# A two-layer hybrid decoder step: prompt attention and 12 of the prompt's first-MLP panels moved ahead of and between the samples' cache work

## The chip, the cores and the metric

One core of a Trainium2 chip runs one launch of the program. The time is device time in microseconds (us). Before the change it is the median of three runs: 1191.11 us, from 1184.08 to 1191.2. Everything is fp32.

## The reference

The step computes two decoder layers for one prompt of 256 tokens and for 8 samples with one new token each (1024 tokens of past in paged caches). Both groups use the same weights, but have their own conditioning vector. D is 1024, the MLP width 4096. Cut to what matters:

```python
for layer in range(2):
    for x, c in ((xp, c_prompt), (xs, c_sample)):
        shift, scale, gate = adaln(c, ada_w, ada_b)      # silu(c) @ w + b, three parts of 1024
        h = rms_norm(x, g) * (1 + scale) + shift
        if layer == 0:
            mq, mk, mv, nq, kc, vc, ks, vs, kw, vw, gt = attn_project(h, w_in, qk_g)   # 2840 columns
            # samples: keys and values are the cache pages and the new token
            o_moba = top 3 of the blocks of 256 keys by mean key, and the own block; 8 heads
            o_cmp, o_sel = compressed blocks of 32 (small MLP), and selected blocks of 64; 8 heads
            o_win = window of 512
            o = concat(o_moba, g0 * o_cmp + g1 * o_sel + g2 * o_win)
            x = x + gate * (o @ w_out)
        else:
            x = x + gate * s5_mixer(h)                   # diagonal complex state space, GLU
    for x, c in both:
        shift, scale, gate = adaln(c, mlp_ada_w, mlp_ada_b)
        h = rms_norm(x, g) * (1 + scale) + shift
        x = x + gate * (square(relu(h @ w1)) @ w2)       # 1024 -> 4096 -> 1024
```

It returns x of both groups, the new cache entries, the window state and the S5 states.

## The kernel before, in words

The program is written by hand as five instruction streams: PE (matrix products), DVE and ACT (vector and activation work), POOL (issues the weight loads), and SP (issues the cache loads). Each stream stands in the order in which it runs, and semaphores tie them. No scheduler moves anything.

Weights come through a ring of four slots of 2 MB (`ring`, `SLOTS` = 4). From the first MLP on each slot's place is cut into panels of 1 MB (`panels`). Cache pages come through 8 buffers of 256 KB (`kv`, semaphores `kv_full` and `kv_free`). Activations are kept transposed: `xT` and `hT` hold 8 blocks of 128 features by 264 columns, 256 of the prompt and 8 of the samples. In most products the weights are stationary (128x128) and the 264 columns are moved past them, so prompt and samples share one pass over the weights.

The stages, with their us in the profiled execution:

- 0 to 129: modulation of layer 0 (`ada0`) and the samples' compressed keys and values (L791).
- 129 to 266: input projection in 6 panels, samples' rows (L821) and the prompt's two halves (L827). The samples' queries are spread over partitions (L805). On DVE the loop at L1995 scores the cached MoBA keys: for each pair of pages two products of 128x512 (L2000) and a sum (L2004), 32 times. PE does the modulation of the first MLP (`ada1`, L702) beside it.
- 266 to 281: gate sums (L854), choice of blocks, softmax of the samples' MoBA branch.
- 281 to 367: `moba_pv` rounds 0 to 7 (L924), each over 8 value pages; from round 3 on POOL issues the odd pages (L548) and SP the even ones (L413). DVE does the query and key norms of the prompt (L1938 to L1956). Modulation of the S5 layer (`ada2`) runs between rounds 0 to 2; prompt attention for MoBA head pairs 0 to 3 between the later ones: `pair_scores` (L967, L968), `pair_log` (DVE L2090 to L2094), the exponential (ACT L1622), `pair_scale` (DVE L2099 to L2105), `pair_rest` on PE (turns L643, values L1006 and L1007).
- 367 to 440: 24 units of selected and window keys: four transposes (`turn_keys`, L643), then 16 small products (`score_keys`, L1061).
- 440 to 490: prompt pairs 4 to 11 (one NSA head each), with two units of selected values (`selected_pv`, L1156) in each, then window values.
- 492 to 532: output projection over all 264 columns (L1203), 8 chunks; sums of squares (L715); norm.
- 532 to 656: first MLP matrix w1 (L1219), 16 panels of 2 chunks, 8 matmuls a chunk. DVE squares the result (`squares`, L2247) and computes the S5 tables in the holes (L2262 to L2386): the angles, after ACT's sine the discretised coefficients, the masked B blocks (`times` L2299, `masked` L2309), the C table and its three lags (L2377 to L2382). `rows_turn`, `c_turn` and `b_turn(0..2)` on PE stand behind w1 panels (`mlp_first`, L1232).
- 656 to 780: second matrix w2 (L1228), 16 panels, with `b_turn(3)` and `k_turn` (L1314) behind its first groups.
- 780 to 936: S5 and GLU (L1444). 936 to 1171: MLP of layer 1, the same two loops. End at 1178.2.

## Time and profile before

| | us |
|---|---|
| median of 3 runs | 1191.11 |
| lowest, highest | 1184.08, 1191.2 |
| span of the profiled execution | 1178.2 |
| PE busy in it | 1019.0 (86%) |
| DVE busy | 423.6 (36%) |
| ACT busy | 248.7 (21%) |
| POOL busy | 137.7 (12%) |
| moved from and to HBM | 210.63 MB read, 7.48 MB written |

The span is from the first to the last instruction that the profiler recorded. The profiled execution's own time as the runs are timed isn't given apart; the median lies 12.9 us above the span. Busy times of PE are those of matmuls; weight loads (PEld) overlap them. The clock of PE is given as granted share, 1.00 or 0.50 in short stretches.

### The profile page before, as it was taken

What the parts mean: (1) busy time and instruction counts of PE and PEld (TensorE: products, weight loads), DVE (VectorE), ACT (ScalarE), POOL (GpSimd) and SP (SyncE); (2) the same over time, 40 slices, a digit from 0 to 9 for tenths busy, and PEclk for the clock granted to TensorE, in tenths of its full rate; (3) what the DMA queues carried; (4) which work ended last, traced back from release to release, by engine and by line L of the source; (5) the groups of instructions that cost most, each with busy time, mean ns of one, the idle gap of its engine ahead of it and who ended that gap; (6) DMA issues with size and microseconds to landing.
All of it is one profiled execution on the core that took longest, in us unless ns stands there. A gap on an engine that the chain in (4) does not pass through costs nothing.

```text
span 1178.2 us, 21097 instructions
## 1 busy us (share of the span) xinstructions
PE 1019.0 (86%) x8404; PEld 751.0 (64%) x8404; DVE 423.6 (36%) x901; ACT 248.7 (21%) x538; POOL 137.7 (12%) x180
## 2 busy tenths in 40 slices
PE   4867999945886869989999999974789799999998
PEld 2646533432234655667888888854668588878886
DVE  0434039887132635424993200048711300000000
ACT  3344121112033424312133320040110211100001
POOL 2000000101023210000111111111121011111110
PEclk9779989986896758998999999987799899999999
DMA  9984449999884492308544443354264344443440
GB/s 322 347 284 118 180 153 319 361 330 356 343 283 136 139 352 71 88 15 234 173 143 144 143 143 120 131 179 146 79 196 133 108 136 149 143 142 131 155 142 37
DMA packets 105580, 215.12 MB, mean 183 GB/s; under 512 B 20560, under 2 KB 53136, under 8 KB 105401
## 3 DMA queue, kind: packets, MB, share of 16 engines
q0 software_dynamic: 40160, 153.20, 38.4%
q1 hardware_dynamic: 63434, 57.81, 15.5%
q10 hardware_dynamic: 1904, 2.94, 0.7%
q8 instruction: 61, 1.00, 0.4%
q14 instruction: 21, 0.17, 0.0%
HBM read 210.63 MB, written 7.48 MB: 185 GB/s over the span
## 4 chain that ended last, share of the span: by engine, by line
PE 72%; DMA 9%; DVE 8%; issue 5%; ACT 3%; SPq 2%; DVEq 0%; POOL 0%; ACTq 0%; POOLq 0%
PE psum L1219 20%; PE psum L1228 20%; DMA sb_arena<-in_cache_moba_kv 6%; PE psum L1444 5%; PE psum L643 4%; PE psum L791 3%; PE psum L1203 2%; PE psum L827 2%; DVE sb_sq L2000 2%; DVE sb_sq L2004 2%; PE psum L702 2%; DMA sb_ring<-in_attn_ada_w 1%; PE psum L715 1%; DMA sb_arena<-in_cache_nsa_kv 1%; PE psum L924 1%
## 5 line engine op out<-in xcount | busy, mean ns | idle before, releaser
L1219 PE MATMUL psum<-sb_hT,sb_ring 128*128 128x264 f32 x1024 | 232.6, 390 | 13.3 <-ACT sb_hT L1493 6.8
L1228 PE MATMUL psum<-sb_arena,sb_ring 128*128 128x264 f32 x1024 | 230.8, 388 | 2.6 <-DVE sb_arena L2247 2.4
L1219 PEld LDWEIGHTS psum<-sb_hT,sb_ring 128*128 128x128 f32 x1024 | 196.6, 193 | 47.5 <-issue 6.8
L1228 PEld LDWEIGHTS psum<-sb_arena,sb_ring 128*128 128x128 f32 x1024 | 195.4, 191 | 36.9 <-issue 3.2
L643 PE MATMUL psum<-sb_cst,sb_arena 128*128 128x128 f32 (+4 forms) x457 | 78.6, 310 | 36.0 <-DMA sb_arena<-in_cache_nsa_kv 9.0
L643 PEld LDWEIGHTS psum<-sb_cst,sb_arena 128*128 128x128 f32 (+4 forms) x457 | 56.0, 156 | 55.0 <-issue 22.6
L2254 DVE SCALAR_TENSOR_TENSOR sb_xT<-psum,sb_mods,sb_xT 128x256 f32<-128x256 f32 (+1 forms) x16 | 7.7, 484 | 224.9 <-PE psum L1228 224.9
L827 PE MATMUL psum<-sb_ring,sb_hT 128*128 128x512 f32 (+1 forms) x192 | 79.4, 566 | 0.0
L2247 DVE TENSOR_TENSOR sb_arena<-sb_arena x16 | 19.7, 1256 | 126.5 <-ACT sb_arena L1728 107.6
L827 PEld LDWEIGHTS psum<-sb_ring,sb_hT 128*128 128x128 f32 x192 | 35.5, 190 | 44.2 <-issue 39.9
L579 POOL DMA_DIRECT2D sb_ring<-in_mlp_w x28 | 24.8, 885 | 310.7 <-issue 147.9
L1444 PE MATMUL psum<-sb_sq,sb_ring 128*128 128x264 f32 x256 | 58.1, 386 | 0.0
L1444 PEld LDWEIGHTS psum<-sb_sq,sb_ring 128*128 128x128 f32 x256 | 48.6, 190 | 8.2
L586 POOL DMA_DIRECT2D sb_ring<-in_mlp_w x32 | 28.3, 885 | 212.1 <-PE psum L1228 147.6
L702 PE MATMUL psum<-sb_ring,sb_cT 128*32 128x512 f32 x288 | 41.7, 683 | 11.5 <-DMA sb_ring<-in_attn_ada_w 10.3
L2000 DVE TENSOR_TENSOR sb_sq<-sb_arena 128x512 f32<-128x512 f32 x64 | 41.9, 689 | 10.8 <-DMA sb_arena<-in_cache_moba_kv 4.9
L924 PE MATMUL psum<-sb_arena 128*32 128x512 f32 x128 | 37.1, 697 | 6.6 <-DMA sb_arena<-in_cache_moba_kv 6.3
L2004 DVE TENSOR_REDUCE sb_sq<-sb_sq 128x1024 f32 x32 | 39.0, 1220 | 4.8 <-DVE sb_sq L2000 1.3
L1916 DVE COPY sb_arena<-psum 64x256 f32<-64x256 f32 x64 | 27.3, 427 | 34.2 <-PE psum L643 33.1
L1712 ACT COPY sb_arena<-psum 32x2048 f32<-32x2048 f32 x16 | 29.7, 1858 | 27.5 <-PE psum L643 27.2
L1728 ACT ACTIVATE sb_arena<-psum 128x264 f32 x32 | 12.5, 391 | 103.1 <-PE psum L1219 103.1
L791 PE MATMUL psum<-sb_arena,sb_ring 128*128 128x256 f32 x128 | 30.4, 402 | 1.0 <-ACT sb_arena L1517 1.0
(422 smaller groups left out, 1110.2 us busy)
## 6 DMA issues: line engine op xcount, KB each, us to landing
sb_ring<-in_mlp_w POOLq DMA_DIRECT2D x64, 1024.0 KB, 6.0
sb_arena<-in_cache_moba_kv SPq DMA_DIRECT2D x108, 256.0 KB, 7.1
sb_ring<-in_attn_ada_w POOLq DMA_DIRECT2D x6, 2048.0 KB, 22.2
sb_ring<-in_mlp_ada_w POOLq DMA_DIRECT2D x6, 2048.0 KB, 11.5
sb_ring<-in_ssm_ada_w POOLq DMA_DIRECT2D x6, 2048.0 KB, 17.6
sb_ring<-in_mlp_ada_w POOLq DMA_DIRECT2D x12, 1024.0 KB, 6.8
sb_ring<-in_attn_w_in POOLq DMA_DIRECT2D x5, 2048.0 KB, 11.3
sb_arena<-in_cache_nsa_kv SPq DMA_DIRECT2D x64, 128.0 KB, 2.9
```

Source lines behind the costliest of these rows:

```text
L586: pool.dma_start(panels[:, j, :].rearrange("p (f c) -> p f c", f=8), w2[:, 8 * j:8 * j + 8, DS(it * 256, 256)]).then_inc(mlp_full_at[j], 16)
L643: return nc.tensor.transpose(out, in_, ident[0:rows, 0:rows])
L702: last = mm(mm_banks[i % len(mm_banks)][group(k), 0:512], cT[:, k, :], ring[:, seq % SLOTS, 512 * k:512 * k + 512], start=(k < 4), stop=(k ...
L791: last = mm(bank[kind][:, 0:256], w1k[kind][:, i, :], at(pairs[:, 4096 * kind + P * i:], (2048, 2), (1, P)), start=(i == 0), stop=(i == CM ...
L827: last = mm(bank[3 * (p % 2) + t][:, 0:w], hT[:, k, P * t:P * t + P], ring[:, seq % SLOTS, w * k:w * k + w], start=(k == 0), stop=(k == KC ...
L924: mm(bank[5][rows, 0:512], p_of(half, r // 2, pg), kv[:, seq % KVS, :], start=(r == 0 and pg < 2), stop=(r == 7 and pg == 7)).then_inc(kv_ ...
L1219: last = mm(bank[m % 4][:, 0:T], panels[:, j, 256 * k + P * ch:256 * k + P * ch + P], hT[:, k, :], start=(k == 0), stop=(k == KC - 1))
L1228: last = mm(bank[2 * pair + c][:, 0:T], panels[:, j, 256 * f + P * c:256 * f + P * c + P], actT[:, 8 * j + f, :], start=(j == 0 and f == 0 ...
L1444: last = mm(bank[b][:, 0:T], panels[:, seq % SLOTS, 256 * k + P * zi:256 * k + P * zi + P], yT[:, k, :], start=(k == 0), stop=(k == KC - 1))
L1712: nc.scalar.copy(BT[32 * i:32 * i + 32, e].rearrange("p r k n -> p (r k n)"), psum[32 * e:32 * e + 32, 4:8, :].rearrange("p a c -> p (a c) ...
L2000: tt(prod[:, 512 * (pg % 2):512 * (pg % 2) + 512], kv[:, pg, :], qb[:, DS(b, 1), :].rearrange("p b c -> p (b c)"), ALU.mult).then_inc(kv_f ...
L2004: last = red(sraw_b[:, DS(b, 1), 8 * (pg - 1):8 * (pg + 1)].rearrange("p b c -> p (b c)"), prod.rearrange("p (h d) -> p h d", d=64), AX, A ...
```

## The change

The program computes the same. What moves:

1. **Weight ring.** Three slots of 2 MB in place of four, and after them units of 1 MB in four places (`UNITS`), issued in the order of one list (`ORDER`, `plan()`). Both compression matrices share one slot. The fourth slot's space holds work buffers (`upper`).
2. **Cache loads.** All MoBA value pages and selected keys are issued by SP; POOL's `odd_values` and `odd_keys` are gone.
3. **Prompt attention.** Pairs 0 to 3 stand between the input panels on PE, and between the page pairs of the scoring on DVE, whose loop is unrolled (`score(first, end)`). The prompt's query and key norms stand ahead of the scoring. Pairs 4 to 11 stand with `moba_pv(0..7)`, one round a pair.
4. **Output projection apart.** The prompt's (256 columns, 4 units) follows the value rounds; the samples' is done after their window values, from 4 units loaded again, with the weights as moving operand (`rows_of_samples`, 256 columns a matmul) and turned back by `turn_rows`.
5. **First MLP.** `w1_first(m)` does chunk m. Chunks 0 to 11 stand in the keys' loop, one behind every second unit, chunks 12 to 19 between the selected and window values, 20 to 23 by the samples' projection, all with 256 columns. Chunks 24 to 31 have 264 columns. The samples' part of the first 12 panels comes from 12 units that are loaded again (`w1_s`). ACT squares the result behind its relu in place of DVE's `squares(0)`.
6. **Second matrix.** `c_turn`, `b_turn(0..3)` and `k_turn` stand behind w2 panels 0, 1, 2, 3, 5 and 7. `ada2` is done in 12 halves behind panels 8 to 15 (`ada2_half`, `ada2_turn`). DVE's `first_mlp_out` stands between the lags of the C table.

In the diff's PE part, cut:

```diff
-            for i in range(5, 12):
-                pair_scores(i)
-                def two_units():
-                    selected_pv(2 * (i - 4))
-                    selected_pv(2 * (i - 4) + 1)
-                pair_rest(i - 1, two_units)
...
+            w_in_samples(3)
+            w_in_prompt(3, 0)
+            pe.wait_ge(N.qk_ev, 4)
+            pair_scores(0)
+            w_in_prompt(3, 1)
+            pair_turn(0)
+            ada1(2)
+            pair_values(0)
+            pair_scores(1)
...
+            for i in range(4, 12):
+                if i < 11:
+                    pair_scores(i + 1)
+                pair_turn(i)
+                cmp_probs_turn(i)
+                moba_pv(i - 4)
+                pair_values(i)
...
+            def w1_first(m, cols=TP):
+
+                if m % 2 == 0:
+                    unit_wait("w1_0", m // 2)
+                w, c = panels[:, UNIT["w1_0", m // 2] % UNITS, :], P * (m % 2)
+                if m >= 2:
+                    pe.wait_ge(N.relu_ev, 4 + m - 1)
+                for k in range(KC):
+                    if m == 0:
+                        pe.wait_ge(N.h_ready, 8 + k + 1)
+                    last = mm(w1_bank(m)[:, 0:cols], w[:, 256 * k + c:256 * k + c + P], hT[:, k, 0:cols],
+                              start=(k == 0), stop=(k == KC - 1))
+                last.then_inc(N.mm_done, 1)
...
+            for n in range(25):
+                beside_keys(n)
+                if n < 24:
+                    turn_keys(n)
+                if n == 1:
+                    pe.wait_ge(N.q_bc_ev, 9)
+                if n:
+                    score_keys(n - 1)
+                    if n % 2 == 0:
+                        w1_first(n // 2 - 1)
...
+            for m in range(24, 32):
+                w1_first(m, T)
+                if m == 25:
+                    rows_turn()
+                if m % 2:
+                    for i in range(3):
+                        first_layer_of_samples(3 * ((m - 25) // 2) + i)
...
+            for n in range(16):
+                it, j = n // UNITS, n % UNITS
+                if j == 0 and it >= 2:
+                    pe.wait_ge(N.out_free, 8 + 2 * it - 2)
+                w2_panel(unit_wait("w2_0", n), j, it % 2)
+                if n == 0:
+                    c_turn()
+                elif n in (1, 2, 3, 5):
+                    b_turn((1, 2, 3, 5).index(n))
+                elif n == 7:
+                    k_turn()
+                    pe.wait_ge(N.s5_b_ev, 4 * LAG + 1)
+                    pe.wait_ge(N.s5_c_ev, LAG)
+                if n >= 8:
+                    for i in range((3 * (n - 8)) // 2, (3 * (n - 7)) // 2):
+                        ada2_half(i)
```

On DVE and on the loads:

```diff
+            score(0, 8)
+            dve.wait_ge(N.bias_back, 16)
+            pair_log(0)
+            score(8, 10)
+            pair_scale(0)
+            score(10, 12)
...
+                if m == 1:
+                    first_mlp_out(0)
+                    times(bbar, 12)
+                    masked(2)
+                    dve.wait_ge(N.s5_bd, 3)
...
-            load_ada(SEQ["ada2"], I["ssm_ada_w"][0])
-            for r in range(3, TS):
-                odd_values(r)
-            for u in range(1, 16, 2):
-                odd_keys(u)
...
+            for i in range(4):
+                load_rows("out", i, w_out)
+            for j in range(10):
+                load_rows("w1_0", j, w1)
+            for i in range(4):
+                load_rows("out_s", i, w_out)
```

DVE, where the MoBA keys are scored. Before, the products (two of 128x512) and their sum stand in a loop, and nothing else:

```order
L1990 MEMSET sb_arena 128x2048
L1995 UNCONDITIONAL_BRANCH
L1995 ISA
L1999 ISA
L2000 ISA
L2000 TENSOR_TENSOR sb_sq<-sb_arena 128x512 x2
L2003 REGISTER_ALU
L2004 ISA
L2004 TENSOR_REDUCE sb_sq<-sb_sq 128x16
```

After, DVE, the same place, behind the eighth page pair:

```order
L2255 TENSOR_TENSOR sb_ring<-sb_arena 128x512 x2
L2257 TENSOR_REDUCE sb_ring<-sb_ring 128x16
L2228 SCALAR_TENSOR_TENSOR sb_arena<-psum,sb_arena 128x2x256
L2229 SCALAR_TENSOR_TENSOR sb_arena<-psum,sb_arena 128x2x128
L2231 TENSOR_REDUCE sb_arena<-sb_arena 128x2
L2232 TENSOR_REDUCE sb_arena<-sb_arena 128x2
L2255 TENSOR_TENSOR sb_ring<-sb_arena 128x512 x2
L2257 TENSOR_REDUCE sb_ring<-sb_ring 128x16
```

`pair_log` (L2228 to L2232) now stands between two page pairs of the scoring (L2255, L2257), and so does `pair_scale` later.

PE, the loop over selected and window keys. Before, turns (L643) and scores (L1061) alternate:

```order
L643 MATMUL psum<-sb_cst,sb_arena 128x128 x4
L1061 MATMUL psum<-sb_arena 32x8 x16
L903 MATMUL psum<-sb_ones,sb_arena 32x1 x4
L1107 MATMUL psum<-sb_arena 32x128 x4
L643 MATMUL psum<-sb_cst,sb_arena 128x128 x4
L1061 MATMUL psum<-sb_arena 32x8 x16
```

After, PE, the first units of the loop:

```order
L670 MATMUL psum<-sb_cst,sb_arena 128x128 x8
L1161 MATMUL psum<-sb_arena 32x8 x16
L670 MATMUL psum<-sb_cst,sb_arena 128x128 x4
L1161 MATMUL psum<-sb_arena 32x8 x16
L1219 MATMUL psum<-sb_hT,sb_ring 128x256 x8
L1184 MATMUL psum<-sb_arena,sb_ring 128x8 x4
```

Behind every second unit (L670, L1161) there now stands one w1 chunk of eight matmuls with 256 columns (L1219 of the changed kernel).

PE, the second matrix (w2). Before, panels (L1228) in groups of four, a B turn (L643) and the k turn (L1314) between them:

```order
L1228 MATMUL psum<-sb_arena,sb_ring 128x264 x64
L643 MATMUL psum<-sb_cst,sb_arena 128x128 x16
L1228 MATMUL psum<-sb_arena,sb_ring 128x264 x64
L1314 MATMUL psum<-sb_ring,sb_arena 32x96 x64
L1228 MATMUL psum<-sb_arena,sb_ring 128x264 x64
L715 MATMUL psum<-sb_sq,sb_ones 128x256 x4
```

After, PE, from behind the fourth panel of w2 (L1353): the last two B turns (L670), the k turn (L1422), ada2 halves (L1363) and their turn (L1374); the C turn and B turns 0 and 1 stand the same way behind the first three panels:

```order
L670 MATMUL psum<-sb_cst,sb_arena 128x128 x16
L1353 MATMUL psum<-sb_arena,sb_ring 128x264 x32
L670 MATMUL psum<-sb_cst,sb_arena 128x128 x16
L1353 MATMUL psum<-sb_arena,sb_ring 128x264 x32
L1422 MATMUL psum<-sb_ring,sb_arena 32x96 x64
L1353 MATMUL psum<-sb_arena,sb_ring 128x264 x16
L1363 MATMUL psum<-sb_ring,sb_cT 16x256 x8
L1353 MATMUL psum<-sb_arena,sb_ring 128x264 x16
L1363 MATMUL psum<-sb_ring,sb_cT 16x256 x16
L1374 MATMUL psum<-sb_cst,sb_arena 32x9 x16
```

The turns that stood behind w1 panels stand behind single w2 panels, and ada2 has moved from the value rounds to w2's second half.

## Rows read from the trace of the kernel before

**Rows 1.** The page's head: span, busy engines, granted clock in 40 slices.
```profile
span 1178.2 us, 21097 instructions
PE 1019.0 (86%) x8404; PEld 751.0 (64%) x8404; DVE 423.6 (36%) x901; ACT 248.7 (21%) x538; POOL 137.7 (12%) x180
...
PEclk9779989986896758998999999987799899999999
```

**Rows 2.** Windows: length; busy PE, PEld, DVE, ACT, POOL; clock, DMA share, GB/s.
```profile
174.00:266.00 92.00, 75.79 (x516) 32.37 (x508) 80.33 (x96) 12.66 (x23) 7.61 (x8) 0.91 0.92 329
285.00:360.00 75.00, 57.96 (x510) 21.92 (x502) 25.84 (x52) 16.79 (x48) 16.89 (x30) 0.91 0.87 310
390.00:400.00 10.00, 9.48 (x344) 7.33 (x343) 6.36 (x17) 7.00 (x11) 3.76 (x7) 1.00 0.74 206
410.00:418.00 8.00, 6.91 (x157) 5.23 (x160) 1.91 (x4) 4.27 (x8) 5.28 (x6) 0.50 0.57 180
532.00:656.00 124.00, 123.73 (x580) 105.95 (x581) 80.30 (x192) 30.94 (x48) 13.87 (x16) 0.98 0.56 172
656.00:780.00 124.00, 123.15 (x689) 104.78 (x691) 11.35 (x31) 20.05 (x19) 14.44 (x17) 1.00 0.41 136
```

**Rows 3.** Chain of waits: start us, length us, engine, what, count.
```profile
519.97 3.57 PE psum L1203 x16
...
656.69 28.72 PE psum L1228 x128
...
687.15 28.48 PE psum L1228 x128
```

**Rows 4.** DVE by form: busy us, mean ns, idle before, releasers.
```profile
L2000 DVE TENSOR_TENSOR sb_sq<-sb_arena 128x512 f32<-128x512 f32 x64 | 41.9, 689 | 10.8 <-DMA sb_arena<-in_cache_moba_kv 4.9 <-ACT sb_arena L1560 3.9 <-DVE sb_sq L2004 1.0
L2004 DVE TENSOR_REDUCE sb_sq<-sb_sq 128x1024 f32 x32 | 39.0, 1220 | 4.8 <-DVE sb_sq L2000 1.3
```

**Rows 5.** DVE timeline: start us, us, operation; scoring, norms, one prompt pair.
```profile
173.37 1.29 DVE L2000 TENSOR_TENSOR sb_sq<-sb_arena 128x512 f32<-128x512 f32 x2 [3.88 <-ACT sb_arena L1560]
...
279.93 1.22 DVE L1938 TENSOR_TENSOR sb_sq<-sb_arena 128x1024 f32<-128x1024 f32 x1
...
288.15 2.36 DVE L1956 TENSOR_TENSOR sb_arena<-sb_arena 128x1024 f32<-128x1024 f32 x2
...
461.96 0.18 DVE L2099 RECIPROCAL sb_arena<-sb_arena 128x4 f32<-128x4 f32 x1 [1.93 <-ACT sb_arena L1622]
...
464.95 0.68 DVE L2094 TENSOR_REDUCE sb_arena<-sb_arena 128x2 f32<-128x512 f32 x1
...
467.56 0.18 DVE L2099 RECIPROCAL sb_arena<-sb_arena 128x4 f32<-128x4 f32 x1 [1.93 <-ACT sb_arena L1622]
```

**Rows 6.** DMA issues (KB, us to landing), and what an issue costs SP (ns).
```profile
sb_ring<-in_mlp_w POOLq DMA_DIRECT2D x64, 1024.0 KB, 6.0
...
L413 SPq DMA_DIRECT2D sb_arena<-in_cache_moba_kv x108: 332/333/1014, 113.0 to 347.6; - x108
```

**Rows 7.** PE timeline: a modulation panel; key steps at two clocks.
```profile
194.21 1.92 PE L702 MATMUL psum<-sb_ring,sb_cT 128*32 128x512 f32 x16
...
394.62 0.66 PE L643 MATMUL psum<-sb_cst,sb_arena 128*128 128x128 f32 x4
...
395.58 0.66 PE L643 MATMUL psum<-sb_cst,sb_arena 128*128 128x128 f32 x4
...
414.47 1.12 PE L643 MATMUL psum<-sb_cst,sb_arena 128*128 128x128 f32 x4
...
416.06 1.12 PE L643 MATMUL psum<-sb_cst,sb_arena 128*128 128x128 f32 x4
```

**Rows 8.** DVE timeline of the S5 tables: after the sine, lags' first and last.
```profile
548.80 0.19 DVE L2277 TENSOR_TENSOR sb_arena<-sb_arena 128x32 f32<-128x32 f32 x1 [1.94 <-ACT sb_arena L1740]
...
591.49 0.69 DVE L2377 TENSOR_TENSOR sb_ring<-sb_ring,sb_arena 128x512 f32<-128x512 f32 x1 [0.16 <-DVE sb_ring L2369]
...
613.94 0.69 DVE L2382 TENSOR_TENSOR sb_ring<-sb_ring,sb_sq 128x512 f32<-128x512 f32 x1
```

More of the change, by code:

```diff
@@ L841, in _, with ada1, turn @@
-            ada(1, bank[6:7], bank[7], first=5)
+            def ada1(i):
+                if i == 0:
+                    pe.wait_ge(N.q_bc_ev, 8)
+                ada(1, bank[6:7], bank[7], first=i, end=i + 1)
+            def turn(groups, n0, banks):
+                for g, pieces in enumerate(groups):
+                    if g >= 2:
+                        pe.wait_ge(N.qk_ev, n0 + g - 1)
+                    for i, piece in enumerate(pieces):
+                        last = tr(banks[g % 2][:, P * i:P * i + P], piece)
+                    last.then_inc(N.qk_tr, 1)
```

1507 lines of the change are left out of this document (846 added, 661 removed).

## The prediction

> **What bounds the kernel now.** I read the page's head, then the stages in windows, then the chain of waits, then single engines in the stages that the change touches. The page says that TensorE (PE) is busy 1019.0 of 1178.2 us, and its 40 slices of the granted clock that of the eight slices at 0.7 or below six lie ahead of 442 us [rows 1]. The windows sort this. In the two MLP stages PE is busy 123.7 and 123.2 of 124 us at full clock: nothing but less PE work shortens them. From 174 to 266 us VectorE (DVE) is busy 80.3 of 92 us: it scores the cached keys, and the stage ends with it. From 285 to 360 neither is full (PE 58, DVE 26 of 75 us) and DMA is at 0.87. In the key loop PE is idle in part, and its clock is 1.00 from 390 to 400 and 0.50 from 410 to 418 [rows 2]. The chain has the output projection at 3.57 us a chunk, and the second MLP matrix (w2) from 656.69 us [rows 3]. So the change moves full-clock PE work out of a stage that PE bounds (532 to 656) into stages that DVE, DMA and short waits bound. The question is what those stages charge for it.
>
> Times below are those of the profiled execution, whose span is 1178.2 us [rows 1]. Its own total isn't given apart; the median of the runs is 1191.11, so I add 12.9 us to a span for what lies around it.
>
> **A. Scoring.** Before, one page pair costs 2 x 0.689 + 1.220 us [rows 4] and with gaps 2.7; 32 of them run from 173.37 [rows 5] to 266.0, the end of that window. Now DVE does the query and key norms ahead of them (279.93 to 290.51, 10.6 us [rows 5]), and behind PE's second compression layer and sooner input panels I add 7: start 191. Into the scoring come four prompt pairs. A pair is 3.67 us of DVE (461.96 to 465.63 [rows 5]), 3.5 without the gate multiply that the first four lack: 14. The NSA norms are three quarters of the 10.6, 8, and the copies and small key norm some 5. With 3 us for waits: 191 + 32 x 2.68 + 14 + 13 + 3 = 306.8. The end of scoring moves by +40.8. PE has its input panels and the pairs underneath and is not the bound.
>
> **B. Gate to values.** Before, the gate and the first softmax end just ahead of 279.93 [rows 5], 13.9 us behind the scoring. After: 306.8 + 13.9 + some 3.5 for compressed prompt attention on DVE = 324, when pair 4 starts.
>
> **C. Eight pairs with eight value rounds.** The loop of pairs alone takes 5.60 (461.96 to 467.56 [rows 5]). Values: a round is 8 pages of 256 KB. Issue costs SP 0.333 us each [rows 6], 2.7 us, so that SP alone doesn't bound it. The stage moved 310 GB/s from 285 to 360 [rows 2], at which 2.1 MB take 6.8; I take 7.0. 7 x 7.0 + 5.5 for the fill + 7.5 for the first page's landing and the last values = 62: 386. This is where the removal of the POOL loads of odd pages acts.
>
> The rows show several issuers but not that they move more. The Trainium skill, "Trainium Kernel Development and Optimization", Key Constraints, says that the issuing queues share the same DMA engines and that several issuers only save issue time; by it giving up POOL costs nothing here. If the row of 310 GB/s had leaned on POOL, a round would be nearer 9 and the sum 14 us more, which is rival 3.
>
> **D, E. Output projection and norm.** Eight chunks at 256 columns instead of 264: 3.57 x 256/264 = 3.45 [rows 3], and the squares between them .5: 31.5, ending at 418. Norm and the wait for its first row: before, PE's projection ends at 523.5 [rows 3] and its first MLP window starts at 532 [rows 2], 8.5 us; with 1.5 for ACT's other work in front, 10: 428.
>
> **F. Keys with 12 chunks.** A key step at full clock is 0.96 us (394.62 to 395.58), at half clock 1.59 (414.47 to 416.06) [rows 7]. I take full clock, since eight-matmul chunks stand between the steps: 24 x 0.96 = 23, small pieces 5, chunks 12 x 3.45 = 41.4, waits 3.6: 501.
>
> The two steps lie in windows of clock 1.00 (390 to 400) and 0.50 (410 to 418) [rows 2]. The Trainium skill, "TensorE: Matmul & The Clock Gate", Part 1, has it that throttled is the default state and activity releases it, on which these rows and my choice agree; a stage that stayed at the low level would give 513 in place of 501.
>
> **G, H.** Selected and window values 10 us, 8 chunks 27.6, waits on softmax between them 5.3: 544. Sample projection: 4 one-MB units of 8 narrow matmuls. The nearest row is the modulation panel, 16 of the same width in 1.92 us [rows 7], so 0.95 each: 3.8. Four chunks 13.8, turns 2.4. The 4 MB of window state and the S5 inputs start at the same point as the weights, and I give 8 us for that: 572.
>
> **I. The last 8 chunks with the samples' own 12 panels.** Per pair of chunks 7.12, three units 2.85, turns 1.3; 4 MB of weights must land in it, each in 6.0 us median [rows 6], and at 310 GB/s 4.2 MB take 13.5. So 13.5 each, 54: w2 starts at 626. Before: 656.69 [rows 3]. Up to here the change is 30.7 us ahead.
>
> **J. w2 gives it back.** PE: 16 x 7.12 = 114. Moved in: one C and four B turns; one is the gap from 685.41 to 687.15 in the chain [rows 3], 1.75, five are 8.75, ada2 12 x 0.95 = 11.4 and its turns 2.7; kept: k turn 3.8, squares 4.4. Sum 145. Stalls: B turn 0 waits for the C table. Before, this chain ran from the sine's result at 548.80 to 591.3 (the first lag starts at 591.49), 42.5 us, and the three lags to 614.6 at 7.8 each [rows 8]. Now the sine follows chunk 29 at about 609, so the table is ready at 651, while PE asks at 641: 10. B turn 2 waits for a lag, the first output chunks' evacuation and the mask: 6.5. B turn 3: 5. Ada2's DMA beside w2's, 2.5 MB per 8.9 us, 4. End: 626 + 145 + 25.5 = 796.5. Before, the window that w2 fills ends at 780 [rows 2]. +16.5.
>
> **K.** Ada2's evacuation stands ahead of the last output chunks, and the late modulation panels of layer 1 start behind fewer free slots: +4. The rest I leave alone.
>
> Sum: 1178.2 + 16.5 + 4 = 1199, and with 12.9: 1212 us. The bill another way: +16 MB of weights; +16 units x 0.95 and +8 row turns x 0.45 = 19 us of PE, less 0.11 x 32 = 3.5 for narrower chunks; ada2 and turns no longer lie under DMA waits. The gain is only what idle PE time (17 us of 75 in 285 to 360, the small gaps between key steps, the half clock) takes up, and the scoring's 40 us eats most of it.
>
> **Bounds of what the trace doesn't show.** Waits inside F to I: 0 (all covered by chunks) to 25. Landing of the 3 sample units: 11.3 (PE alone) to 18 (3 x 6.0) a group, -9 to +18 in all. S5 stalls in J: 0 if the sine comes early, to 40 if DVE's evacuations queue in front. Start of scoring: 184 (norms only) to 198.
>
> **Rivals.**
> 1. *PE-bound after all, faster.* The chunks are without dependence, so they fill every softmax wait: 17 us of waits in F to H vanish, E's wait falls to 2 (-8), the S5 stalls go (-20 of 25.5). 1212 - 45 = 1167. For it: the MLP windows run at 99.8% busy with the S5 chain beside them [rows 2]. Against: DVE's chain is serial and starts 50 us later.
> 2. *Even.* Half of these waits vanish: 1190.
> 3. *Values starve.* SP alone issues everything, for the selected keys four pieces a unit with page registers between; if rounds are 9 us and keys run at the low clock: +14 + 12 = 1238. For it: the stage's DMA share of 0.87 [rows 2] was reached with two issuers. Against: 0.333 us an issue [rows 6].
> 4. *PE isn't ready with a pair's scores* when DVE comes to them, so DVE waits in the midst of the scoring: +10, part of my own range.
>
> **Chances.** A measurement here tells about 1% from no change: below 1179 or above 1203. My sum and rival 3: slower 0.54 (0.46 + 0.08). Even: 0.21. Rival 1: 0.25. Range: from rival 1 to rival 3, 1168 to 1238; the likeliest alone has 1200 to 1226.
>
> **What would show it.** Last scoring reduction at 307 (right if within 6); value rounds at 7.0; last output chunk at 418; w2's first matmul at 626; in w2 a PE wait of some 10 us in front of a turn, released by DVE's masked C; w2's end at 796. Wrong if scoring ends before 295, if w2 starts before 610, or if the w2 stage holds no wait over 3 us.

## The result, and the profile after

The changed kernel takes 1262.44 us in the median of four runs (1258.54 to 1262.9), the kernel before 1191.15. The ratio is 1.061, 95% interval 1.056 to 1.066: slower by 6%. The forecast was slower, 1212, with a range up to 1238. The sign is right and the size is not. One of the four runs of the variant e5 below took 1340.7 us at a granted clock of 0.79 instead of 0.90, and the ratios leave such slow runs out.

The page of the changed kernel: its span, busy engines, granted clock and the chain by engine.

```profile
span 1260.6 us, 22175 instructions
PE 1045.9 (83%) x9012; PEld 765.8 (61%) x9012; DVE 413.5 (33%) x890; ACT 259.1 (21%) x557; POOL 131.3 (10%) x152
...
PEclk9779979896699989859878889998689989999999
...
PE 60%; DVE 13%; DMA 11%; SPq 7%; issue 6%; ACT 3%; POOL 0%; ACTq 0%; DVEq 0%; POOLq 0%
```

Against [rows 1] PE is busy 27 us more, of which the forecast's bill had 19 less 3.5. The span grew by 82. The new thing is that 7% of the chain (some 88 us) is SPq, the queue of SyncE: the engine that issues the cache loads is on the path that sets the end.

The windows of the changed kernel: length; busy PE, PEld, DVE, ACT, POOL; clock, DMA share, GB/s.

```profile
200.00:313.00 113.00, 81.15 (x658) 42.35 (x656) 103.01 (x150) 35.13 (x80) 11.30 (x12) 0.86 0.92 321
...
334.00:402.00 68.00, 65.38 (x322) 28.89 (x324) 26.25 (x65) 22.71 (x76) 0.00 (x0) 0.97 0.69 224
...
445.00:516.00 71.00, 70.19 (x1043) 57.28 (x1036) 13.74 (x30) 20.71 (x42) 5.28 (x6) 0.98 0.51 150
516.00:580.00 64.00, 35.68 (x311) 25.58 (x310) 6.07 (x18) 3.72 (x10) 1.78 (x3) 0.73 0.41 119
580.00:690.00 110.00, 82.27 (x768) 60.97 (x767) 22.41 (x80) 20.35 (x39) 21.70 (x24) 0.86 0.83 261
690.00:864.00 174.00, 153.10 (x1118) 124.26 (x1118) 62.72 (x149) 38.32 (x35) 24.68 (x28) 0.94 0.53 178
```

Read them with [rows 2]. The scoring (200 to 313) is DVE's by its busy time, 103 of 113 us; the DMA share of 0.92 stands beside it, and no run here tries which of the two would give way. In the value rounds (334 to 402) PE counts as busy for 65 of 68 us, a share that hides waits (see e3). The keys with their chunks (445 to 516) are PE's, 70 of 71 at clock 0.98: this part of the change does what it says. Then PE falls to 36 of 64 us with no other engine busy and DMA at 0.41 (516 to 580): the selected values. From 580 to 690 PE is idle for 28 us beside a DMA share of 0.83. In the w2 stage it is idle for 21.

A ledger in us, by the forecast's own letters; "after" is read from the first or last matmul or reduction of the part, and the error is the difference of the durations:

| part | forecast ends at | after ends at | forecast length | length | error |
|---|---|---|---|---|---|
| A scoring | 306.8 | 313.3 | | | +6.5 |
| B, C gate, pairs 4 to 11, values | 386 | 402.6 | 79.2 | 89.3 | +10.1 |
| D prompt's projection | 418 | 433.2 | 31.5 | 30.6 | -0.9 |
| E norm | 428 | 445.0 | 10 | 11.8 | +1.8 |
| F keys with 12 chunks | 501 | 516.0 | 73 | 71.0 | -2.0 |
| G selected and window values, 8 chunks | 544 | 590.5 | 43 | 74.5 | +31.5 |
| H samples' projection, 4 chunks | 572 | 620.7 | 28 | 30.2 | +2.2 |
| I 8 chunks, 12 units | 626 | 691.0 | 54 | 70.3 | +16.3 |
| J w2 | 796.5 | 864 | 170.5 | 173 | +2.5 |
| K rest | 1199 | 1260.6 | 402.5 | 396.6 | -5.9 |

The errors add to 62 us of span. Half of it is one line, G. Of B and C, the first value product starts 22.7 us after the scoring's end, and each round then takes 8.2 us from start to start where the forecast had 7.0.

The chain of waits of the changed kernel in G: start us, length us, engine and line. L398 reads page numbers into registers, L449 issues one of the four 64 KB pieces of a unit.

```profile
502.65 0.33 SPq L449
503.12 0.47 SPq L398
503.62 0.15 SPq L398
503.89 0.15 SPq L398
504.24 0.47 SPq L398
504.71 0.36 issue
505.74 0.34 SPq L449
506.28 0.33 SPq L449
506.81 0.33 SPq L449
507.33 0.33 SPq L449
```

A unit is 4.3 us of SP, of which the four issues are 2.1 (0.53 from one to the next) and the reading of page numbers about 2.2. Nothing in this stretch waits for memory. SP's own timeline shows the whole row, first of the changed kernel, then of the kernel before: start us, length us, issues.

```profile
395.61 76.55 SPq L449 DMA_DIRECT2D sb_arena<-in_cache_nsa_kv  x64
472.38 15.75 SPq L456 DMA_DIRECT2D sb_arena<-in_state_nsa_win  x8
...
492.38 68.59 SPq L449 DMA_DIRECT2D sb_arena<-in_cache_nsa_kv  x64
561.19 5.63 SPq L456 DMA_DIRECT2D sb_arena<-in_state_nsa_win  x8
```

```profile
392.31 8.95 SPq L430 DMA_DIRECT2D sb_arena<-in_state_nsa_win  x8
404.20 71.76 SPq L423 DMA_DIRECT2D sb_arena<-in_cache_nsa_kv  x64
476.18 6.45 SPq L430 DMA_DIRECT2D sb_arena<-in_state_nsa_win  x8
```

The 72 us of selected values were there before. They ran from 404 to 476 under the end of the keys and the eight prompt pairs (440 to 490). The change took these 50 us of cover away, put them over the MoBA values, and left 8 chunks (28 us) in their place. Only two of the eight (at 517 and 528 us) stand ahead of the last unit of selected values; the other six start at 563.7, when the waits are over. Dealing them out among the units was not tried. And the loads start later against the keys' end: value unit 0 needs the buffer of window unit 0, the 17th of 24 key units, and each pair of key units now takes 5.5 us with its chunk.

PE's side of it in the changed kernel, the selected-value matmuls (L1238): start us, length us, and in brackets the idle time before.

```profile
545.38 0.65 PE L1238 MATMUL psum<-sb_arena 128*32 128x128 f32 x8 [2.59 <-DMA sb_arena<-in_cache_nsa_kv]
549.63 0.65 PE L1238 MATMUL psum<-sb_arena 128*32 128x128 f32 x8 [3.60 <-DMA sb_arena<-in_cache_nsa_kv]
553.89 0.66 PE L1238 MATMUL psum<-sb_arena 128*32 128x128 f32 x8 [3.60 <-DMA sb_arena<-in_cache_nsa_kv]
558.24 0.66 PE L1238 MATMUL psum<-sb_arena 128*32 128x128 f32 x8 [3.69 <-DMA sb_arena<-in_cache_nsa_kv]
```

A unit every 4.3 us, SP's pace. "DMA" is named as releaser, but the DMA share is 0.41: it is the issue that came late. From 516 to 580 us PE waits ten times for selected values, 27.8 us in all; in the kernel before, from 440 to 490 us, it doesn't wait for them once. Behind two of these waits a chunk takes 6.3 and 5.5 us instead of 3.7 (granted clock 0.58 and 0.66 over them).

### The profile page after: what moved, and what is told of

It is laid out like the page before. It is cut to its first block, busy times and chain, and to the rows that moved or that the text cites. A ratio compares the mean times of both kernels' runs of the same rounds, so it can differ in the third digit from the quotient of the medians.

```text
span 1260.6 us, 22175 instructions
## 1 busy us (share of the span) xinstructions
PE 1045.9 (83%) x9012; PEld 765.8 (61%) x9012; DVE 413.5 (33%) x890; ACT 259.1 (21%) x557; POOL 131.3 (10%) x152
## 4 chain that ended last, share of the span: by engine, by line
PE 60%; DVE 13%; DMA 11%; SPq 7%; issue 6%; ACT 3%; POOL 0%; ACTq 0%; DVEq 0%; POOLq 0%
PE psum L1353 15%; PE psum L1345 9%; PE psum L1219 7%; PE psum L1573 5%; DMA sb_arena<-in_cache_moba_kv 4%; PE psum L857 4%; DMA sb_ring<-in_mlp_w 4%; PE psum L670 3%; SPq L398 3%; PE psum L817 2%; PE psum L1134 2%; SPq L449 2%; DVE sb_ring L2255 2%; DMA sb_arena<-in_cache_nsa_kv 1%; DVE sb_ring L2257 1%
## 5 line engine op out<-in xcount | busy, mean ns | idle before, releaser
L1353 PE MATMUL psum<-sb_arena,sb_ring 128*128 128x264 f32 x1024 | 234.4, 391 | 6.1 <-DMA sb_ring<-in_mlp_w 2.7
L1353 PEld LDWEIGHTS psum<-sb_arena,sb_ring 128*128 128x128 f32 x1024 | 196.1, 193 | 41.6 <-issue 5.4
L1219 PE MATMUL psum<-sb_hT,sb_ring 128*128 128x256 f32 (+1 forms) x512 | 129.2, 413 | 6.3 <-DMA sb_ring<-in_mlp_w 6.3
L670 PE MATMUL psum<-sb_cst,sb_arena 128*128 128x128 f32 (+4 forms) x457 | 77.8, 309 | 54.9 <-DMA sb_arena<-in_cache_nsa_kv 13.2
L1345 PE MATMUL psum<-sb_hT,sb_ring 128*128 128x264 f32 x512 | 116.8, 392 | 6.6 <-ACTq L1948 6.6
L1219 PEld LDWEIGHTS psum<-sb_hT,sb_ring 128*128 128x128 f32 x512 | 103.7, 206 | 25.4 <-DMA sb_ring<-in_mlp_w 7.8
L1345 PEld LDWEIGHTS psum<-sb_hT,sb_ring 128*128 128x128 f32 x512 | 99.0, 194 | 24.0 <-ACTq L1948 6.7
L670 PEld LDWEIGHTS psum<-sb_cst,sb_arena 128*128 128x128 f32 (+4 forms) x457 | 57.0, 156 | 76.8 <-issue 26.3
L577 POOL DMA_DIRECT2D sb_ring<-in_mlp_w x28 | 24.7, 883 | 275.8 <-PE psum L1134 133.4
L1847 ACT ACTIVATE sb_arena<-psum 128x256 f32<-128x256 f32 (+1 forms) x32 | 12.3, 385 | 165.4 <-PE psum L1219 165.4
L2507 DVE TENSOR_TENSOR sb_arena<-sb_arena x8 | 10.1, 1258 | 108.7 <-ACT sb_arena L1952 108.7
L2255 DVE TENSOR_TENSOR sb_ring<-sb_arena 128x512 f32<-128x512 f32 x64 | 41.7, 687 | 5.5 <-DMA sb_arena<-in_cache_moba_kv 4.6
L2514 DVE SCALAR_TENSOR_TENSOR sb_xT<-psum,sb_mods,sb_xT 128x256 f32 x8 | 3.9, 484 | 111.1 <-PE psum L1353 111.1
L2257 DVE TENSOR_REDUCE sb_ring<-sb_ring 128x16 f32<-128x1024 f32 x32 | 39.0, 1220 | 1.1
L729 PE MATMUL psum<-sb_ring,sb_cT 128*32 128x512 f32 x192 | 27.7, 703 | 11.4 <-DMA sb_ring<-in_attn_ada_w 10.7
```

The source lines that it names most:

```text
L670: return nc.tensor.transpose(out, in_, ident[0:rows, 0:rows])
L729: last = mm(mm_banks[i % len(mm_banks)][group(k), 0:512], cT[:, k, :], ring[:, seq % SLOTS, 512 * k:512 * k + 512], start=(k < 4), stop=(k ...
L1219: last = mm(w1_bank(m)[:, 0:cols], w[:, 256 * k + c:256 * k + c + P], hT[:, k, 0:cols], start=(k == 0), stop=(k == KC - 1))
L1345: last = mm(bank[m % 4][:, 0:T], panels[:, j, 256 * k + P * ch:256 * k + P * ch + P], hT[:, k, :], start=(k == 0), stop=(k == KC - 1))
L1353: last = mm(bank[2 * pair + c][:, 0:T], w[:, 256 * f + P * c:256 * f + P * c + P], actT[:, 8 * j + f, :], start=(j == 0 and f == 0), stop= ...
L2255: tt(prod[:, 512 * (page % 2):512 * (page % 2) + 512], kv[:, page, :], qb[:, b, :], ALU.mult).then_inc(kv_free[page], 1)
```

## The experiments

A caution for all of them. The end of the scoring lies between 313.3 and 326.5 us in the twelve profiles of the changed kernel and its variants, none of which alters the scoring; what moves it isn't known. Timed runs of one kernel differ by up to 16 us (e13: 1181.78 to 1198.26). So a single part is judged by the length of its stage, against the scatter of that stage in variants whose edit doesn't touch it: first to last MoBA value product 60.6 to 64.2 us, first to last selected value 55.2 to 57.0, last window value to w2 116.7 to 121.1, w2 163.1 to 166.4, S5 with GLU 162.2 to 164.8, the first-MLP matmuls of layer 1 115.6 to 117.1.

A total that leaves the scoring's scatter out is the time from the end of the scoring to the end of the span. It is 947.3 us in the changed kernel; the variants' are shorter by 24.1 (e1), 30.3 (e2), 1.1 (e3), 19.8 (e5), 4.4 (e7), 44.5 (e8), 44.0 (e9), 8.2 (e10) and 9.2 us (e12), and longer by 3.2 (e4) and 8.6 (e11). Each ratio is against the kernel before on the same chip; the changed kernel itself has 1.061. The intervals of e9, e10 and e11 are the widest, 0.024 to 0.027.

### SP's issue time (e2, e1, and e6 on the kernel before)

e2, page numbers read once:

```diff
-            nsa_units(KV_SV, 384, lambda r, u: in_turn(r * 16 + 2 * u), range(KVS))
+            same = in_turn(0)
+            nsa_units(KV_SV, 384, lambda r, u: same, range(KVS))
```

> The changed kernel, but SP reads the page numbers of the selected values once ahead of the loop and loads the same four pages in each of the 16 units (this leaves out the choice of the right pages; bytes, DMAs and waits stay). Theory S (SP's issue time is what the selected values wait for: in the changed kernel 64 issues from 492.4 to 561 us, 4.3 us a unit, of which about 2.2 is reading page numbers): a unit takes about 2.1 us, SP ends near 530 instead of 561, PE's waits on in_cache_nsa_kv between 521 and 563 shrink, and the time falls by 22 to 28 us to about 1236. Rival D (the DMA engines or the small 64 KB pieces are the limit): a unit still lands every 4.3 us, the time stays at 1262 within 3.

Measured: 1242.45 us, ratio 1.046 (1.043 to 1.049). SP's timeline:

```profile
499.59 40.54 SPq L449 DMA_DIRECT2D sb_arena<-in_cache_nsa_kv  x64
```

The same 64 issues in 40.5 us instead of 68.6. The first to the last value matmul takes 28.5 us instead of 55.9. The gain of 27 us in the stage (20 in the total) comes with all bytes and pieces in place, so rival D falls.

e1, two issuers (four semaphores were merged into others so that POOL's loads could have their own):

```diff
-            nsa_units(KV_SV, 384, lambda r, u: in_turn(r * 16 + 2 * u), range(KVS))
+            nsa_units(KV_SV, 384, lambda r, u: in_turn(r * 16 + 2 * u), range(0, KVS, 2))
...
+            def odd_selected(v):
+                low, high = (pages_at(2 * v + first, 2, mybir.EngineType.Pool) for first in (0, 4 * PAGES))
+                found = [p for pair in zip(low, high) for p in pair]
+                pool.wait_ge(kv_free[v % KVS], v // KVS + KV_SV // KVS + 1)
+                for g in range(4):
+                    pool.dma_start(kv[:, v % KVS, g * P:(g + 1) * P], nsa_p[found[g], :, 384:384 + P].rearrange("n p c -> (n p) c")
+                                   ).then_inc(odd_full[v % KVS], 16)
```

> The changed kernel with the odd units of the selected values issued by POOL, SP keeping the even ones. Same result, same bytes. Theory S: two issuers of 8 units each, SP some 34 us, the time falls by 18 to 28 us to about 1239; less if POOL's issues stand in the way of its own weight loads. Rival D: no gain, 1262 within 3.

Measured: 1246.27 us, ratio 1.049 (1.046 to 1.053). First to last value matmul 31.2 us instead of 55.9. Its window from 516 to 580:

```profile
516.00:580.00 64.00, 50.17 (x447) 38.33 (x445) 6.27 (x19) 8.11 (x17) 16.97 (x27) 0.85 0.70 189
```

PE 50 of 64 us in place of 36, clock 0.85 in place of 0.73. With the right pages and the same result this is a real repair, worth 25 us of stage and 16 of the total.

e6, the same edit as e2 in the kernel before:

> The kernel before with the page numbers of the selected values read once (the same four pages in every unit; leaves out the choice of the pages). Theory H (in the kernel before SP's 78 us of issuing selected and window values, from 404.2 to 482.6, lie under the prompt pairs 4 to 11 and cost little): the time stays within 3 us of before, ratio 0.997 to 1.003. Rival (SP bounded the kernel before as well): it falls by over 6 us, ratio under 0.995.

Measured: 1188.93 beside 1188.42 us, ratio 1.004 (1.000 to 1.009). SP needs 62.5 instead of 71.8 us for the 64 issues and nothing gains. Theory H stands: before, the same issue time was covered. The edit takes only 9 of the 72 us away here, so this is a weaker trial than e2; that PE doesn't wait for a selected value in this kernel says the same. It became a cost because its cover was moved.

### The MoBA value rounds (e3)

Every odd page of `moba_pv` issued by POOL, as in the kernel before for rounds 3 to 7:

```diff
-            moba_units(KV_MV, 512, lambda r: in_turn(r * 4, 4), range(KVS))
+            moba_units(KV_MV, 512, lambda r: pages_at(r * 4, 4), range(0, KVS, 2))
...
+            for r in range(TS):
+                odd_values(r)
```

> The changed kernel with the odd pages of all MoBA value rounds issued by POOL as in the kernel before. Theory S for the value rounds (8.6 us a round in the changed kernel, SP reading 8 page numbers for 3.3 us and issuing for 4.2): a round falls to 6.8 to 7.2, the stage from 334 to 402.6 is 10 to 12 us shorter, time about 1251. Rival D (a round is bound by transfer: 256 KB pages at about 240 GB/s): no gain, 1262 within 3. Rival P (the pairs' loop of 5.6 us plus the value matmuls): 8.0 a round, -4.

Measured: 1268.01 us, ratio 1.066 (1.063 to 1.069), no gain. First to last value matmul 61.0 us instead of 63.7, inside the scatter of 60.6 to 64.2. Theory S falls for this stage. So does P, though PE counts as busy for 65 of 68 us. Two rounds of the changed kernel, 16 value products each:

```profile
343.68 5.26 PE L1067 MATMUL psum<-sb_arena 128*32 128x512 f32 x16
...
362.35 2.07 PE L1067 MATMUL psum<-sb_arena 128*32 128x512 f32 x16
```

Both at full clock. In the second the pages are there, and its round takes 6.55 us (361.32 to 367.87). In the first most products wait for their page: the pages land mostly 0.63 to 0.68 us apart, a product's record is 0.6 us long, and so almost no idle time shows. Five of the eight rounds are of this kind, with products over 4.5 to 6.3 us; by that some 16 of the 63.7 us are waits for pages. PE's own work is 6.5 us a round, and SP's own 7.4 (from 338.07 to 345.51, without a wait). With two issuers the pages still land up to 8.2 us after their issue, and PE still waits. What is left is rival D or the round trip through the eight buffers, a page being issued only when the one before it in its buffer is used; the mean DMA share of 0.69 speaks against D alone. No run separates the two.

### The stretch from the last window value to w2 (e4, e7, e10, e11, e12, and e13 on the kernel before)

It is 119.2 us long in the changed kernel (571.8 to 691.0). PE's timeline of the changed kernel there, waits in brackets; L1113 are the samples' units, L1219 the first-MLP chunks:

```profile
599.61 1.93 PE L1113 MATMUL psum<-sb_ring,sb_arena 128*32 128x256 f32 x16 [6.36 <-DMA sb_ring<-in_attn_w_out]
...
640.58 1.93 PE L1113 MATMUL psum<-sb_ring,sb_arena 128*32 128x256 f32 x16 [10.75 <-DMA sb_ring<-in_mlp_w]
...
661.59 7.39 PE L1219 MATMUL psum<-sb_hT,sb_ring 128*128 128x264 f32 x32 [1.80 <-DMA sb_ring<-in_mlp_w]
...
675.47 9.07 PE L1219 MATMUL psum<-sb_hT,sb_ring 128*128 128x264 f32 x32 [2.80 <-DMA sb_ring<-in_mlp_w]
```

e4, the copy of the window state (4 MB, at 612.7 us) moved behind the wait for the S5 states:

```diff
-            sp.dma_start(O["win_sample"][0, :, 0:511].rearrange("b t a k d -> b (t a k d)"),
-                         I["state_nsa_win"][0, :, 1:512].rearrange("b t a k d -> b (t a k d)")).then_inc(N.y_stored, 16)
             sp.wait_ge(N.fin_ev, 2)
+            sp.dma_start(O["win_sample"][0, :, 0:511].rearrange("b t a k d -> b (t a k d)"),
+                         I["state_nsa_win"][0, :, 1:512].rearrange("b t a k d -> b (t a k d)")).then_inc(N.y_stored, 16)
```

> The changed kernel with the 4 MB copy of the window state issued by SP behind the S5 states instead of at 612.7 us. Theory C (the copy takes the DMA engines from the first-MLP units): PE's wait of 10.75 us at 629.8 goes, time falls by 8 to 12 to about 1252. Rival U (the units themselves, 4 MB a group of two chunks, are what the engines can't bring sooner): the wait stays, time 1262 within 3.

Measured: 1268.79 us, ratio 1.067 (1.063 to 1.072). The stretch is 111.7 us, 7.5 shorter, as expected of theory C. But the S5 and GLU stages after w2 are 172.9 instead of 162.3 us: 10.6 given back, about half of it in one wait of PE for a GLU weight (5.18 us), and the total doesn't fall. The expectation forgot that the new place has its own loads.

e12, the copy left out altogether:

```diff
-            sp.dma_start(O["win_sample"][0, :, 0:511].rearrange("b t a k d -> b (t a k d)"),
-                         I["state_nsa_win"][0, :, 1:512].rearrange("b t a k d -> b (t a k d)")).then_inc(N.y_stored, 16)
...
-            sp.wait_ge(N.y_stored, 16 * 6)
+            sp.wait_ge(N.y_stored, 16 * 5)
```

> The changed kernel without the 4 MB copy of the window state (leaves out that output). Moved behind the S5 states (e4) the copy gave 7 us back between the window values and w2 and took 11 in the S5 stage, and ahead of the units (e11) it made a wait of 21 us. Theory C3 (the copy costs DMA time wherever it stands beside a ring of four slots that PE follows closely): without it window end to w2 start falls by 7 and nothing is taken later, total 1252 to 1256. Rival: no gain, the waits come from the round trip of the slots alone.

Measured: the stretch is 110.6 us, 8.6 shorter, and S5 with GLU is 162.2, unchanged. The total doesn't follow: 1266.39 us (1258.15 to 1266.49), ratio 1.067 (1.060 to 1.073). In its profile the scoring ended at 326.5, 13 us later than in the changed kernel's, in a part that doesn't differ. Counted from the end of the scoring it is 9.2 us shorter. C3 is borne out by the stage and by this count (7 to 9 us); the timed total doesn't show it. The same edit in the kernel before:

> The kernel before without the same copy (leaves out that output). There it starts at 537 us beside the first MLP, whose PE windows from 552 on are 20.0 of 20 us busy. If the wide PE stage hides it, the time stays within 3 us of before; C3 would then say that the change has moved the copy from a covered place to an uncovered one. Rival: it falls by 5 to 8 us, the copy costs the same in both.

Measured: 1189.81 beside 1185.46 us, ratio 1.004 (1.000 to 1.008): no gain, the copy is free there. The traces say how. In the kernel before, the copy is issued at 537.0, and the next 1 MB panel, issued at 543.9, lands after 19.5 us; later in the same stage a panel takes 6.1. But PE has three other panels of 7.1 us to do between a panel's issue and its use, and never waits in these 122 us. In the changed kernel the copy is issued at 612.7, and the unit issued at 613.8 lands after 26.7 us, while PE has 16 us of work ahead of it (to 629.8): the wait of 10.75 us. That wait stands in every variant with the copy in this place and its whole load (10.3 to 11.1 us in e1, e2, e3, e5, e9 and e10), and in none without (e4, e8, e12).

e11, the S5 table loads cut to one row:

```diff
+                if n >= 4:
+                    dst, src = dst[0:1], src[0:1]
                 sp.dma_start(dst, src).then_inc(N.s5_rows_loaded if n < 4 else N.s5_loaded, 16)
```

> The changed kernel with the eight S5 table loads (B and C, from 582 to 612 us on SP) cut to their first row (leaves out the rest of the S5 tables). Theory C2 (these loads of many small pieces share the DMA engines with the units of the samples' projection and make PE's waits of 6.4 us at 593 and 10.75 us at 630): window end to w2 start falls by 8 to 14 us, and the total by as much. Rival: the waits are the round trip of the four slots, under 3 us.

Measured: 1273.71 us, ratio 1.077 (1.064 to 1.091): slower, against both theories. Its PE timeline:

```profile
616.76 1.94 PE L1115 MATMUL psum<-sb_ring,sb_arena 128*32 128x256 f32 x16 [21.18 <-DMA sb_ring<-in_attn_w_out]
```

SP was done with the S5 loads sooner and issued the 4 MB copy at 590.1 instead of 612.7, just ahead of the samples' last projection unit, which then took over 20 us to arrive. The stretch grew to 130.2. So the edit removed one load and moved another into a worse place: it says little on the S5 loads themselves, and much on the copy. The unit issued ahead of the copy, at 586.3, lands after 6.0 us; its like in the changed kernel, issued at 583.9 among the S5 loads, after 7.8. And the wait of 6.36 us at 593 isn't the copy's, since e12 still has 5.10 there. How it divides between S5 loads and round trip isn't shown.

e7, the samples' first-MLP units loaded to one eighth:

```diff
-                pool.dma_start(unit_slot(n, KC), by_rows(w)[:, :, 256 * (i % 16):256 * (i % 16) + 256]).then_inc(unit_full_at[n % UNITS], 16)
+                ks = slice(0, 1) if name == "w1_s" else slice(0, KC)
+                pool.dma_start(unit_slot(n, KC)[:, ks, :], by_rows(w)[:, ks, 256 * (i % 16):256 * (i % 16) + 256]).then_inc(unit_full_at[n % UNITS], 16)
```

> The changed kernel with only one eighth of each of the samples' 12 reloaded first-MLP units loaded (leaves out the other seven eighths of these weights; matmuls, waits and order stay). Theory U (between 590 and 690 us the loads of weights set the pace, DMA share 0.83): PE's waits on in_mlp_w of 10.75 + 0.8 + 0.4 + 1.8 + 2.8 us go for the most part, w2 starts 12 to 17 us sooner counted from the last window value, time 1248. Rival R (PE's own work and the turns through ACT set it): under 4 us.

Measured: 1262.37 us, ratio 1.066 (1.057 to 1.076). The stretch is 115.3 us, 3.9 shorter and 1.4 below the scatter of the unchanged ones, at the edge of rival R. 11 MB less bring 4 us at most: bytes are not what sets the pace. In its timeline the waits ahead of the panels stay (1.54, 1.62 and 4.47 us), and the panels behind them take 10.17, 10.41 and 9.86 us, against 7.4 at full clock (the granted clock over them is 0.70 to 0.74).

e10, another order in the ring:

```diff
+WS_AT = ((0, 2), (2, 4), (4, 6), (6, 12))
...
-        order += [("w1_0", j)] + [("w1_s", 3 * (j - ALONE) + i) for i in range(3)]
+        order += [("w1_0", j)] + [("w1_s", i) for i in range(*WS_AT[j - ALONE])]
```

> The changed kernel with the samples' 12 units behind the last four first-MLP panels as 2, 2, 2, 6 instead of 3, 3, 3, 3. Theory R (with one panel and three units a group in four slots, each panel goes into the slot of the panel before it, is issued when that one is done, lands some 6 us later, and PE has 3 units of 1.1 us to cover it: waits of 1.80, 2.80 and 2.04 us, and behind each a panel at the low clock, 9 to 10 us instead of 7.1): with two units a group a panel's slot is free earlier, the waits ahead of the panels go, and window end to w2 start falls from 119 to 107 to 113; the tail of six units gives 3 back. Rival U (bytes of weights bound it): no change, since the bytes are the same.

Measured: 1262.82 us, ratio 1.067 (1.055 to 1.080). The stretch is 118.2 us: no change. Of the panels' waits one is gone and one is 2.02, but the tail of six units waits 3.97, 2.26 and 0.60 us. Theory R's detail (the panel's own slot) isn't refuted, but what the order saves at one place it pays at the other. It gains elsewhere, which neither theory foresaw: the w2 matmuls take 158.4 us instead of 166.2. The last w1 chunk now ends 18 us before w2 begins, not 6, and B turn 0 no longer waits for DVE (4.03 us before).

What follows for the stretch: of the 18 us that H and I went over the forecast, 7 to 9 belong to the copy, 4 at most to the units' bytes, and the rest to a ring of four slots whose loads are issued only when a slot is free. The first of a group lands about 6 us later and each further one some 3 us behind it, while PE has 1.1 us of work for a unit. That last share is a remainder, not measured by itself.

### The turns in w2 (e5)

```diff
-                elif n in (1, 2, 3, 5):
-                    b_turn((1, 2, 3, 5).index(n))
-                elif n == 7:
+                elif n in (2, 3, 5, 7):
+                    b_turn((2, 3, 5, 7).index(n))
+                elif n == 8:
```

> The changed kernel with the four B turns behind w2 panels 2, 3, 5, 7 (were 1, 2, 3, 5) and the k turn behind 8 (was 7). The waits in front of the B turns are 4.0, 0.6, 6.2 and 3.0 us in the changed kernel, and each is followed by matmuls at the low clock. Theory T (PE asks for the tables before DVE has them): these waits fall to under 4 us in all, the w2 stage falls from 166 to 154, time about 1251. Rival (DVE's chain is what ends the stage, whatever the order): w2's end stays.

Measured: 1247.07 us, ratio 1.055 (1.043 to 1.066). The w2 matmuls take 144.1 us from first to last instead of 166.2. PE's timeline, first of the changed kernel (L670 are the turns), then of e5:

```profile
714.23 3.54 PE L670 MATMUL psum<-sb_cst,sb_arena 128*128 128x128 f32 x16 [4.03 <-DVEq L2636]
...
740.78 3.68 PE L670 MATMUL psum<-sb_cst,sb_arena 128*128 128x128 f32 x16 [6.21 <-DVE sb_arena L2581]
...
761.91 3.61 PE L670 MATMUL psum<-sb_cst,sb_arena 128*128 128x128 f32 x16 [2.96 <-DVE sb_arena L2581]
```

```profile
717.73 1.91 PE L670 MATMUL psum<-sb_cst,sb_arena 128*128 128x128 f32 x16
...
743.39 1.91 PE L670 MATMUL psum<-sb_cst,sb_arena 128*128 128x128 f32 x16
...
759.38 1.91 PE L670 MATMUL psum<-sb_cst,sb_arena 128*128 128x128 f32 x16
```

The waits of 4.03, 0.61, 6.21 and 2.96 us are down to one of 0.61. The gain is larger than the 13.2 us of waits because each of the three long ones was followed by a turn at 3.5 to 3.7 us instead of 1.91: such a wait costs its length and 1.7 us of low clock behind it (granted 0.50 to 0.52 over these turns), 5 us for the three. The first pair of w2 chunks took 10.36 us in the changed kernel and 7.36 in e5, with the same wait of 2 us ahead of both; these 3 us are not the edit's. Theory T stands, and DVE's chain has room.

### Repairs together (e8, e9)

e8 is e1, e5 and the copy moved behind the S5 states and the second relus; e9 is e1, e5 and the ring order of e10.

> The changed kernel with POOL issuing the odd selected values, the B turns later, and the window-state copy moved under the last MLP (behind the S5 states and the second relus). If the three act in different stages their gains add: 16 + 10 + 5 = 31 us, about 1231; still slower than before. If they lean on the same DMA engines or the same DVE chain, under 22.

> The changed kernel with POOL issuing the odd selected values, the B turns later, and the ring order of e10; the window-state copy in its place. By the gains of the single runs (16 and 15) and theory R's 6 to 12: 1222 to 1230, above before by 2.5 to 3.5%. If it is below 1200, the change without its three faults would be about even with before, which I don't expect: the scoring and the w2 stage still carry 45 and 20 us more.

Measured: e8 1224.47 us, ratio 1.036 (1.027 to 1.046); e9 1225.27 us, ratio 1.037 (1.025 to 1.049). The two gains of e1 and e5 add: counted from the end of the scoring 24.1 and 19.8 us, and together 44.0 in e9. In times that is 37 us off 1262, and the 31 that the expectations went by came from single medians. e9 landed in its range of 1222 to 1230 without the 6 to 12 us of theory R. In e8 the copy again cost in its new place: the first-MLP matmuls of layer 1 took 124.8 us instead of 116.8. None of the versions beats the kernel before. What they all carry is the scoring: in e9 it ends at 318.8, before at 266.0, and no run tries to shorten it.

## Why the prediction was right or wrong

**A, right in kind, 6.5 us short.** DVE bounds the scoring (103 of 113 us). The first page pair starts at 201 where I had 191, and the scoring is then 112 us long where I had 116. The end also varies by 13 us between profiles.

**B, C, 10 us short.** I put a round at 7.0 us by transfer. It is 8.2 from start to start. PE's own work is 6.5, more than the pair loop's 5.6, since the values' 2 us come on top, but it isn't what sets the round. The pages' arrival does, as I had it in kind; the size by the stage's mean of 310 GB/s was too small, and e3 shows that a second issuer wouldn't have helped.

**D, E, F, right within 2 us each.** The key loop with its chunks runs at full clock (0.98), as chosen in F. The Trainium skill, "TensorE: Matmul & The Clock Gate", Part 1 (activity releases the clock), agrees with this stage, and with G, where the clock fell to 0.73 as PE waited. The 513 that F names for a stage at the low level is too low: 24 key steps alone add 24 x 0.63 = 15 us, and each chunk would add more (6.3 for 3.7 us at 528).

**G, the step that failed: 31 of 62 us.** The term is the 5.3 us of waits, which were 27.8 for the selected values alone. I wrote "selected and window values 10 us, waits on softmax between them 5.3". I priced what PE does and never asked what SP must issue for it. The one sentence on SP's issue time, in C, took 0.333 us an issue [rows 6] and left out the 0.2 between issues and the reading of page numbers, which are the larger half: 4.3 us a unit and not 1.3. The row that would have told it was in the trace of before (404.20, 71.76 us, 64 issues). Rival 3 named the mechanism (SP alone, selected keys, page registers between) but put it on the selected keys, where PE is busy 70 of 71 us, and on the value rounds, where a second issuer changed nothing beyond the scatter, and gave it 26 us and a chance of 0.08. e2 and e1 settle it, and e6 agrees.

The rule of the Trainium skill that I leaned on in C ("Trainium Kernel Development and Optimization", Key Constraints: several issuers only save the sequencer's issue time) holds in both places. In the value rounds a second issuer gave nothing clear of the scatter. With the selected values, SP's own time, for issuing and for reading page numbers, was what was short, and the second issuer gave 25 us. I had read the "only" as "nothing".

**H, I, 18 us short, nearly all of it in I.** The 8 us for the copy and the S5 loads were the right size for the copy alone, and stood in H, where PE waited 7.6 us for weights; of these 6.5 are there without the copy too (e12). The copy's own 7 to 9 fell into I. A group of I took 17.6 us where I had 13.5, inside my bounds ("11.3 to 18 a group") and near their upper end.

**J, right in the sum (173 for 170.5), in part by luck.** The waits ahead of B turns 2 and 3 are 6.2 and 3.0 (6.5 and 5 forecast); ahead of B turn 0 it is 4.0, not 10, since PE too came later. What I left out is the low clock behind each wait, 5 us at the turns and 3 in the first panels; they make up for the first wait, which was 6 us shorter than forecast. e5 shows the waits and the slow turns together to be 18 of its 22 us. A forecast of stalls should have asked at once whether they could be ordered away.

**The addition at the end.** I added 12.9 us for what lies around the span, taken from a median against one profiled execution. For the changed kernel, the profiled execution took 1262.34 us with a span of 1260.6: 1.7 us lie around it. The 12.9 were mostly the scatter of the runs of before. This hid 11 us of the error: by spans the forecast was off by 62, by times by 50.

**The signs of being wrong.** None of the three that I had named came: scoring before 295, w2 before 610, no wait over 3 us in w2. All looked for a kernel that is faster than forecast. The signs for it, read again: scoring end 313.3 for 307, rounds 8.2 for 7.0, last output chunk 433 for 418, w2 from 691 for 626.

## What to carry to other kernels

When work is moved, list what it was covering, for every queue and not only for the engines that compute: here 72 us of load issues lost 50 us of cover and their own matmuls hadn't changed. Price an issue by the distance from one to the next in the timeline, with the register reads between, and not by its own duration. A wait named "DMA" beside a DMA share of 0.4 was an issue that came late here: look at the issuing queue's timeline. A busy share of 65 of 68 us hid some 16 us of waits: compare a group of matmuls with the same group where its data is there.

## What the runs showed that I had not expected

- Reading page numbers costs SP as much as issuing: 2.2 of the 4.3 us a unit (0.47 us for a load of registers, 0.15 for each step behind it).
- One 4 MB copy is not free merely since the mean DMA share is low. It cost 7 to 9 us between the values and w2, 10.6 beside S5 and GLU and 8 beside the MLP of layer 1 (the DMA share there is 0.42 in the changed kernel), and PE waited 21 us for a unit issued behind it. In four traces (both kernels, e8, e11) the first 1 MB load issued behind the copy, 0.1 to 7 us later, took 19.5 to 26.7 us to land, against 6. In the kernel before, beside the first MLP, this was covered and cost nothing that shows.
- PE waits of 3 to 6 us ahead of a turn nearly doubled the turn's time, from 1.91 to 3.6 us.
